# A two-layer decoder trunk in split fp32: the SwiGLU rows are turned by VectorE blocks and SBUF-to-SBUF transfers in place of TensorE

## The reference

```python
D_MODEL, SEQ, DEPTH, D_FF = 1024, 256, 2, 2816

def swiglu_ffn(h, w_in, w_out):
    g, u = jnp.split(h @ w_in, 2, axis=-1)
    return (jax.nn.silu(g) * u) @ w_out

for l in range(DEPTH):
    x = x + 0.5 * swiglu_ffn(rmsnorm(x, norm_ffn1[l]), ffn1_w_in[l], ffn1_w_out[l])
    ...
    x = x + cross_attention(rmsnorm(x, norm_xattn[l]), rmsnorm(mem, norm_mem[l]),
                            xattn_wq[l], xattn_wkv[l], xattn_wo[l])
    x = x + 0.5 * swiglu_ffn(rmsnorm(x, norm_ffn2[l]), ffn2_w_in[l], ffn2_w_out[l])
return rmsnorm(x, norm_final)
```

## Time and profile before

| | |
|---|---|
| median of 3 runs | 1137.6 us (1137.36 to 1137.78) |
| time of the profiled execution | 1138.02 us |
| its span | 1136.3 us |
| granted TensorE clock, mean | 0.999 |
| TensorE matmuls busy | 1121.5 us (99%) |
| VectorE busy | 680.9 us (60%) |
| ScalarE busy | 543.4 us (48%) |
| GpSimd busy | 26.0 us (2%) |
| DMA | 202.7 MB, 178 GB/s |

### The profile page before, as it was taken

The page is one execution under the profiler, slowest core; times in us unless marked ns, Lnnn a source line. Parts: engine busy times, 40 slices in busy tenths (PEclk is TensorE's granted clock), DMA queues, the critical chain, the costliest instruction groups (busy, mean ns, idle before and its releaser), DMA issues.

```text
span 1136.3 us, 12874 instructions
## 1 busy us (share of the span) xinstructions
PE 1121.5 (99%) x5174; PEld 928.2 (82%) x5174; DVE 680.9 (60%) x767; ACT 543.4 (48%) x599; POOL 26.0 (2%) x23
## 2 busy tenths in 40 slices
PE   8999999999999999999999999999999999999997
PEld 6888888888888888888888888888888888888885
DVE  5555545799655655554565555468996556555542
ACT  5544434755554544443454444347464535444441
POOL 0000000000000000000000000000000000000000
PEclk9999999999999999999999999999999999999999
DMA  7955555543553466555566564555455435555451
GB/s 255 296 167 180 176 174 195 198 174 124 209 185 112 129 204 185 186 185 170 192 196 187 184 188 164 194 193 189 147 186 172 160 113 184 187 184 187 166 192 68
DMA packets 159259, 202.68 MB, mean 178 GB/s; under 512 B 6922, under 2 KB 115030, under 8 KB 159200
## 3 DMA queue, kind: packets, MB, share of 16 engines
q1 hardware_dynamic: 158112, 200.82, 54.0%
q10 hardware_dynamic: 1088, 1.05, 0.3%
HBM read 200.79 MB, written 1.05 MB: 178 GB/s over the span
## 4 chain that ended last, share of the span: by engine, by line
PE 76%; issue 17%; DVE 3%; ACT 3%; DMA 1%; POOL 0%; DVEq 0%; SPq 0%; POOLq 0%; ACTq 0%
PE acc L1244 23%; PE acc L1246 23%; PE acc L1245 23%; PE turn L1142 4%; PE acc L1445 1%; PE acc L1420 1%; DVE w_lo L721 1%; ACT w_hi L400 1%; DMA w_raw<-in_ffn_w_in 1%; DVE arena L908 1%; PE acc L1215 0%; PE acc L1347 0%; PE acc L1216 0%; PE acc L1226 0%; POOL rstd L375 0%
## 5 line engine op out<-in xcount | busy, mean ns | idle before, releaser
L721 DVE TENSOR_TENSOR w_lo<-w_raw,w_hi 128x2048 fp32r<-128x2048 f32 x191 | 428.1, 2246 | 262.3 <-ACT w_hi L400 262.3
L400 ACT CAST w_hi<-w_raw 128x2048 fp32r<-128x2048 f32 x191 | 357.5, 1872 | 137.6 <-PE acc L1246 126.6
L1244 PE MATMUL acc<-w_hi,xT_hi 128*128 128x512 f32 x872 | 346.3, 397 | 0.0
L1246 PE MATMUL acc<-w_hi,xT_lo 128*128 128x512 f32 x872 | 340.4, 390 | 0.0
L1245 PE MATMUL acc<-w_lo,xT_hi 128*128 128x512 f32 x872 | 339.3, 389 | 0.0
L1244 PE MATMUL acc<-w_hi,hT_hi 128*128 128x512 f32 x608 | 241.1, 397 | 0.8 <-DVE hT_lo L893 0.8
L1246 PE MATMUL acc<-w_hi,hT_lo 128*128 128x512 f32 x608 | 237.1, 390 | 0.0
L1245 PE MATMUL acc<-w_lo,hT_hi 128*128 128x512 f32 x608 | 236.7, 389 | 0.0
L1246 PEld LDWEIGHTS acc<-w_hi,xT_lo 128*128 128x128 f32 x872 | 163.7, 188 | 35.3
L1245 PEld LDWEIGHTS acc<-w_lo,xT_hi 128*128 128x128 f32 x872 | 164.0, 188 | 32.1
L1244 PEld LDWEIGHTS acc<-w_hi,xT_hi 128*128 128x128 f32 x872 | 163.8, 188 | 31.6
(11 more groups left out here) (109 smaller groups left out, 497.0 us busy)
## 6 DMA issues: line engine op xcount, KB each, us to landing
w_raw<-in_ffn_w_in SPq DMA_DIRECT2D x174, 512.0 KB, 4.8
w_raw<-in_ffn_w_out SPq DMA_DIRECT2D x80, 512.0 KB, 4.3
w_raw<-in_mix_w_in SPq DMA_DIRECT2D x32, 512.0 KB, 4.5
w_raw<-in_xattn_wkv SPq DMA_DIRECT2D x32, 512.0 KB, 4.3
w_raw<-in_mix_w_out SPq DMA_DIRECT2D x16, 512.0 KB, 4.4
w_raw<-in_xattn_wq SPq DMA_DIRECT2D x16, 512.0 KB, 4.5
w_raw<-in_xattn_wo SPq DMA_DIRECT2D x16, 512.0 KB, 4.2
w_raw<-in_ffn_w_out SPq DMA_DIRECT2D x16, 256.0 KB, 2.8
```

What stands on the lines that cost most here:

```text
L400: act.copy(w_hi[:, u % SLOTS, 0:n], w_raw[:, u % SLOTS, 0:n]).then_inc(w_split_hi, 1)
L721: dve.tensor_tensor(w_lo[:, u % SLOTS, 0:n], w_raw[:, u % SLOTS, 0:n], w_hi[:, u % SLOTS, 0:n].bitcast(F32), ALU.subtract).then_inc(w_spli ...
L1244: pe.matmul(o, hi, wh, start=(first and j == 0), stop=False)
L1246: ins = pe.matmul(o, lo, wh, start=False, stop=(last and j == nk - 1))
```

## The change

The turns of `hact` on TensorE go. In chunk c VectorE now transposes `hact` in blocks of 32x32 (one `transpose` of 128 partitions by 512 elements) into `hblk`, which leaves each block turned but in the wrong quarter of the partitions. GpSimd then issues 16 DMAs from SBUF to SBUF, one for each pair of partition quarters, of 32 partitions by 128 elements (512 bytes a partition, 16 KB), into `hfeat`; after them `hfeat` holds the 256 hidden columns on the partitions, in another order of the free elements. `hT_hi` and `hT_lo` are made from `hfeat` with a reordering read. `hblk` and `hfeat` have two buffers each and lie in `kT`, which the attention uses only between the two SwiGLUs of a layer. ScalarE and VectorE now take chunk c-1 where they took chunk c; the last chunk's parts come after `split_hi` and `split_lo` of unit `base + 2 FC + 4`. The transpose of a chunk waits for the landing of the chunk two before, and the DMAs of a chunk wait for the transpose and, from the third chunk on, for `hT_lo` of the chunk two before. The diff of the ScalarE, VectorE, GpSimd and TensorE lists:

```diff
@@ buffers
+        hblk = kT[:, 0:4, :].rearrange("p (i k) s -> p i (k s)", i=2)
+        hfeat = kT[:, 4:8, :].rearrange("p (i k) s -> p i (k s)", i=2)
...
+        NBLK, RUN, SHUFFLES = P // B, 2 * T * B, 16
+        def chunk_no(l, f, c):
+            return (2 * l + f) * FC + c
+        def hfeat_count(g):
+            return 16 * SHUFFLES * (g // 2 + 1)
@@ gpsimd
+            def shuffle(g):
+
+                pool.wait_ge(hblk_ready, g + 1)
+                if g >= 2:
+                    pool.wait_ge(hT_ready, g)
+                for a in range(NBLK):
+                    for q in range(NBLK):
+                        pool.dma_start(hfeat[B * q:B * q + B, g % 2, a * RUN:(a + 1) * RUN],
+                                     hblk[B * a:B * a + B, g % 2, q * RUN:(q + 1) * RUN]).then_inc(hfeat_landed[g % 2], 16)
+
             inv_sqrt(1, V_X)
+            for c in range(2):
+                shuffle(chunk_no(0, 0, c))
             pool.wait_ge(sgu_landed, 16)
...
             for l in range(L):
                 at = Layer(l)
-                for k, i in enumerate((V_MIX, V_SGU, V_CLN, V_Q, V_F2, V_X)):
+                for c in range(0 if l else 8, FC):
+                    shuffle(chunk_no(l, 0, c))
+                for k, i in enumerate((V_MIX, V_SGU, V_CLN, V_Q, V_F2)):
                     inv_sqrt(at.at(6, 3 + k), i)
+                for c in range(FC):
+                    shuffle(chunk_no(l, 1, c))
+                inv_sqrt(at.at(6, 8), V_X)
@@ scalar, chunk
-                    act.wait_ge(turned, turn_no(at.l, f"f{f + 1}_{c}"))
-                    act.copy(hT_hi[:, 2 * c:2 * c + 2, :],
-                             tb[T_BANK(c)][:, :].rearrange("p (k s) -> p k s", k=2)).then_inc(hT_hi_ready, 1)
+                    if c:
+                        hidden_hi(c - 1)
                     split_hi(base + 2 * c + 5, at)
+                def hidden_hi(c):
+                    g = chunk_no(l, f, c)
+                    act.wait_ge(hfeat_landed[g % 2], hfeat_count(g))
+                    act.copy(hT_hi[:, 2 * c:2 * c + 2, :].rearrange("p k (t a s) -> p k t a s", t=T, a=NBLK),
+                             hfeat[:, g % 2, :].rearrange("p (a k t s) -> p k t a s", a=NBLK, k=2, t=T)).then_inc(hT_hi_ready, 1)
...
-                state["next"] = base + 2 * FC + 4
+                split_hi(base + 2 * FC + 4, Layer(l))
+                hidden_hi(FC - 1)
+                state["next"] = base + 2 * FC + 5
@@ vector, chunk
+                    g = chunk_no(l, f, c)
+                    dve.wait_ge(hact_ready, at.at(4 * FC, T + 2 * FC * f + 2 * c + 2))
+                    if g >= 2:
+                        dve.wait_ge(hfeat_landed[g % 2], hfeat_count(g - 2))
+                    dve.transpose(hblk[:, g % 2, :].rearrange("p (q k t s) -> p t k q s", q=NBLK, k=2, t=T),
+                                  hact[:, :, :].rearrange("p t (k q s) -> p t k q s", k=2, q=NBLK)).then_inc(hblk_ready, 1)
+                    if c:
+                        hidden_lo(c - 1)
                     split_lo(base + 2 * c + 5, at)
@@ tensor
-                def hidden_turn(c, at):
-                    pe.wait_ge(hact_ready, at.at(4 * FC, T + 2 * FC * f + 2 * c + 2))
-                    pe.wait_ge(hT_ready, at.at(2 * FC, 1 + FC * f + c))
-                    turn(T_BANK(c), [(kt * S + t * P, hact[:, t, kt * P:(kt + 1) * P]) for kt in range(2) for t in range(T)])
...
-                    hidden_turn(c - 1, at0)
                     unit(base + 2 * c + 1, at0, c % 3, xT_hi, xT_lo, GK, False, True)
...
-                        if n == 0 and j == 0:
-                            hidden_turn(FC - 1, at0)
```

More of the change, by code:

```diff
@@ L16 @@
 GN = 512
+B = 32
 def trunk_kernel(nc, x, mem, norm_ffn1, ffn1_w_in, ffn1_w_out, norm_mix, mix_w_in, sconv_w, sgu_norm_g,
@@ L69, in chunk_turns @@
     def chunk_turns(l, f):
[L71 to L77, removed]
+        return [EXTRA[c] for c in range(FC) if (l, f) == (0, 0) and c in EXTRA]
     def layer_turns(l):
@@ L91, in turn_no @@
         return T_NO[l, name]
-    TB = {name: i % 2 for i, name in enumerate(x for x in layer_turns(1) if x[:3] not in ("f1_", "f2_"))}
+    TB = {name: i % 2 for i, name in enumerate(x for x in layer_turns(1))}
     TB["next00"], TB["next01"] = 0, 1
     TB["start00"], TB["start01"] = 1, 0
-    def T_BANK(c):
-        return 0
     F1O_PAIR, F2O_PAIR = (2, 0), (2, 1)
@@ L214, in trunk_kernel @@
         gate_ready, hact_ready = sem("gate_ready"), sem("hact_ready")
+        hblk_ready = sem("hblk_ready")
+        hfeat_landed = [sem(f"hfeat_landed{i}") for i in range(2)]
         hT_hi_ready, hT_ready = sem("hT_hi_ready"), sem("hT_ready")
@@ L380, in _ @@
                                pattern=[[0, L * 4], [-1, P]], channel_multiplier=1).then_inc(consts_ready, 1)
+            for c in range(2, 8):
+                shuffle(chunk_no(0, 0, c))
             inv_sqrt(2, V_MEM)
@@ L817, in chunk @@
                 def chunk(c, at):
+                    if chunk_no(l, f, c):
+                        dve.wait_ge(hblk_ready, chunk_no(l, f, c))
                     for t in range(T):
@@ L837, in chunk, with hidden_lo @@
                         steps.link(dve.memset(wT[:, :, 0:PAD_D], 0.0))
+                def hidden_lo(c):
+                    g = chunk_no(l, f, c)
+                    dve.wait_ge(hT_hi_ready, g + 1)
+                    rows = slice(2 * c, 2 * c + 2)
+                    dve.tensor_tensor(hT_lo[:, rows, :].rearrange("p k (t a s) -> p k t a s", t=T, a=NBLK),
+                                      hfeat[:, g % 2, :].rearrange("p (a k t s) -> p k t a s", a=NBLK, k=2, t=T),
+                                      hT_hi[:, rows, :].rearrange("p k (t a s) -> p k t a s", t=T, a=NBLK).bitcast(F32),
+                                      ALU.subtract).then_inc(hT_ready, 1)
                 for c in range(FC):
                     chunk(c, Layer(l))
-                state["next"] = base + 2 * FC + 4
+                split_lo(base + 2 * FC + 4, Layer(l))
+                hidden_lo(FC - 1)
+                state["next"] = base + 2 * FC + 5
             for l in range(L):
```

## The result

| | before | changed |
|---|---|---|
| median | 1137.7 us (4 runs, 1137.4 to 1138.2) | 1117.6 us (4 runs, 1116.3 to 1118.8) |
| ratio to before, 95% interval | | 0.9822 [0.981, 0.9835] |
| span of the profiled execution | 1136.3 us | 1114.6 us |

The account below looks back on a forecast made before the run. TensorE, busy 99%, bounds the kernel; with the change GpSimd's issues set the pace: 1138.0 + 225.6 (issue excess, removed turns included) + 5.4 (clock) = 1369, less 0.4 for the median, 1368 us; range 1116 less some 2 us to 1500.

Parts of the forecast that it names:

- what the turns are worth: On TensorE's list: removing 44 turns of four transposes, 0.50 us each, takes 22.0 us off the path.
- x: On GpSimd's queue: time to issue one DMA, put at 1.06 us, so 16 issues take 17.0 us a chunk.
- the bounds of 0.25 and 2.66: For one GpSimd issue: SyncE's small DMA issue, 0.25 us, as low end; GpSimd's slowest root, 2.66 us, as high.
- the rival: On GpSimd's queue: issues are cheap, under 0.68 us, so the turns' whole 22.0 us come off, 1116 us; 27%.
- The point from which it decides: Issue price above which GpSimd is slower than TensorE's 10.87 us chunk and sets the pace: 0.68 us.
- the ring: Way around from landing through splits, gate and transpose to landing: three chunks, 34 us against 51, so not the pace.
- GpSimd's pace beyond the point: In each SwiGLU, GpSimd's 176 issues set the time: excess 176x - 130.2, 56.4 us, 225.6 us over four.
- second rival: On GpSimd's queue: VectorE's SBUF reads hold issuing up, 5.3 us more a chunk, 1595 us, or 1335 at x = 0.69; 16%.
- The costs put at nothing: On the DMA engines: 512 more packets a chunk, 2.0 us of all 16, a share of 0.18, cost nothing.
- the term of 5.4 us: On TensorE: long pauses may lower its clock to 1.2 GHz, costing 0 to 11 us in four SwiGLUs; middle taken.

Follow-up runs that it names:

- both: The kernel before, turns kept and used, with VectorE's transposes and GpSimd's 704 transfers added, their result unused: 1139.0 us, ratio 1.0.
- no_transfers: The changed kernel without its 704 transfers, hT_hi and hT_lo read from the transposed blocks where they lie: 1116.8 us, ratio 0.9817.
- split32: The changed kernel with all 16 transfers of a chunk cut in two halves of 256 bytes a partition, 32 in all: 1310.6 us.
- same_chunk: The changed kernel with hT_hi and hT_lo of chunk c taken back into chunk c instead of chunk c + 1: 1433.4 us, ratio 1.2587.

## Why the prediction was wrong

- **What bounds the kernel, and what the turns are worth: right.** 0.50 us a turn, 10.87 us a chunk without it; measured 10.88. The sum of 22.0 us stands against 21.7 in the spans and 20.1 and 21.5 in two sets of medians, whose intervals are about 1.5 us to either side.
- **The step that failed is the price of one issue on GpSimd.** The prediction put x at 1.06 us, "the middle row" of GpSimd's reciprocal roots; it is 0.488, so 16 issues take 7.8 us, well inside a chunk, and not 17.0. The roots were the wrong neighbour. They compute on tiles, and their 1.06 and 2.66 seem to hold a wait for VectorE: the root of 1.06 at 813.64 starts 0.17 us behind a VectorE instruction with two SBUF inputs (L981, 64x512, about 0.70) and ends 0.53 us behind it, as the one of 2.66 ends 0.55 us behind a weight split; six of the 14 take 0.69 or 0.70. Even these are dearer than an issue. The true value lay inside the bounds of 0.25 and 2.66, between SyncE's small issue and ScalarE's large one, both of which the prediction had shown. With 704 us of time for each microsecond of x above the deciding point, the sign of the forecast hung on that single choice. The wide range, from 1114, did hold the 1117.6, but only since it was stretched to take in the rival; the forecast and the chances stood on the wrong side.
- **The point from which it decides: partly wrong.** The prediction gave x = 0.68 by pace and called the ring one over three chunks, harmless. It is over two chunks, because the next chunk's gates on ScalarE and its `hact` on VectorE stand behind the splits that stand behind the landing. With 4.0 us from the last issue to the landing (11.83 - 7.81) the point is 2 x 10.88 = 8.65 + 16x + 4.0, so x = 0.57, an estimate from these rows. At 0.488 the changed kernel passes; 20 transfers don't, and with the split moved they do.
- **GpSimd's pace beyond the point: right.** 1310 and 1295 worked out with the measured price, 1310.6 and 1296.3 measured.
- **The hold-up by VectorE (second rival): refuted.** 352 issues in a row take 0.488 each, and in the changed kernel the 16 from 1008.38 take their 7.81 us with a whole weight split of VectorE beside them (below). The root that took 2.66 us is a tile-reading instruction, and it looks held. This agrees with the rule of the Trainium skill (SBUF — State Buffer, "Who interferes with whom"), by which a VectorE instruction with two SBUF inputs contends with a GpSimd instruction that reads SBUF and not with one that only writes it. That an issue is of the second kind no row shows; the rows show that it isn't held. VectorE's row:

```profile
1011.25 2.29 DVE L751 TENSOR_TENSOR w_lo<-w_raw,w_hi 128x2048 fp32r<-128x2048 f32 x1 [1.12 <-ACT w_hi L423]
```

- **The costs put at nothing: right.** The packets and the transpose cost nothing that can be measured (`both`, `no_transfers`).
- **TensorE's clock.** TensorE doesn't pause in the chunks of the changed kernel, so the term of 5.4 us fell away. Where pauses came the clock did fall, which the prediction had left open: in `split32` the half unit behind the last landing starts its first nine matmuls 0.43 us apart (1263.26 to 1266.72 in the last SwiGLU) and then goes back to 0.23, 1.7 us more in all, where the prediction's middle was 5.4 / 4 = 1.35. In `same_chunk` the trace shows the same inside the chunks (TensorE's timeline, the first matmuls behind a pause of 4.81 us):

```profile
1303.95 0.79 PE L1285 MATMUL acc<-w_hi,xT_hi 128*128 128x512 f32 x1 [4.81 <-DVE w_lo L748]
1304.54 0.63 PE L1286 MATMUL acc<-w_lo,xT_hi 128*128 128x512 f32 x1
1304.97 0.63 PE L1287 MATMUL acc<-w_hi,xT_lo 128*128 128x512 f32 x1
...
1307.67 0.40 PE L1285 MATMUL acc<-w_hi,xT_hi 128*128 128x512 f32 x1
1307.90 0.40 PE L1286 MATMUL acc<-w_lo,xT_hi 128*128 128x512 f32 x1
```

Behind the pause matmuls start 0.43 us apart, the 1.2 GHz level, and at 1307.67 they are 0.23 apart again. The kernel's mean clock is 0.908, that of `split32` 0.955.

## What to carry to other kernels

When work moves from a full engine to an idle queue, three points decide: the price of one issue, the pace that it gives against the period of the loop, and the way round through the in-order lists of the engines that wait for it. Trace that last one by list order, not by data: what stands behind the wait belongs to the ring, and taking one instruction out of it (here a weight split, by moving `hT_hi` and `hT_lo` behind it) was worth 23 us at 20 transfers. And where the sign hangs on one unseen price, choose the neighbour that does the same thing (an issue for an issue), not one that only runs on the same engine, and keep both signs in view: the issues of other queues ranged from 0.25 to 0.66 us.

## What the runs showed of the hardware

- A DMA issued by GpSimd, SBUF to SBUF, 32 partitions by 512 bytes, held its queue for 0.488 us; with half the columns 0.488, with half the rows 0.478. The same transfer issued by SyncE took 0.65 us (median of all 704: 0.59), so GpSimd was the cheaper one, while SyncE's DMAs from HBM of a few rows take 0.25.
- 704 such transfers beside 200 MB of weights landed in 3.4 us (median; 1.6 to 6.2) and cost no measurable time. In `same_chunk` the median was 2.0; what makes the difference was not tried.
- GpSimd's queue pauses now and then for 2.5 to 2.7 us with nothing that it waits for: in the changed kernel every seventh chunk (112 issues), with 20 transfers every sixth (120). With 24 transfers and the split moved (`late24`) it is every 120 issues again, for 1.2 to 2.5 us. In `split32`, where the queue is never empty, two of the SwiGLUs show 352 issues in one piece, and the last one a gap of 0.66 us. What it is was not tried.
